# Two Strassen pairs for the query and key projection of the forgetting attention

## The reference, cut to what matters

```python
xn = rms_norm(h, norm_mix[i])
proj = jnp.einsum('bsd,de->bse', xn, w_in[i])
gdn_qkv, gdn_z, gdn_a, gdn_b, fox_qkv, fox_f, merge = split_cols(proj, IN_SPLITS)
...
q_f = rms_norm(fox_qkv[..., :FOX_W].reshape(B, S, FOX_HEADS, FOX_HD), q_norm[i])
k_f = rms_norm(fox_qkv[..., FOX_W:2 * FOX_W].reshape(B, S, FOX_HEADS, FOX_HD), k_norm[i])
v_f = fox_qkv[..., 2 * FOX_W:].reshape(B, S, FOX_HEADS, FOX_HD)
```

## Time and profile before

| | |
|---|---|
| median of 3 runs | 906.24 us (905.82 to 906.25) |
| profiled execution | 906.76 us, span 905.0 us |
| PE busy | 893.1 us, 99% of the span |
| DVE busy | 498.6 us, 55% |
| ACT busy | 198.1 us, 22% |
| DMA | 266 MB, 294 GB/s on the mean |

### The profile page before, as it was taken

One profiled execution on the slowest core, in us unless ns is written; L12 is line 12 of the kernel. 1 busy time (PEld: TensorE's weight loads), 2 busy tenths in 40 slices (PEclk: granted clock), 3 DMA queues, 4 the chain that ended last, 5 costly groups with the idle time before them and its releaser, 6 DMA issues.

```text
span 905.0 us, 21061 instructions
## 1 busy us (share of the span) xinstructions
PE 893.1 (99%) x9194; PEld 510.3 (56%) x9194; DVE 498.6 (55%) x954; ACT 198.1 (22%) x401; POOL 48.1 (5%) x72
## 2 busy tenths in 40 slices
PE   8999999999999999999999999999999999999997
PEld 6888755455845554446555555545455555555543
DVE  3656735964586887866434354443434444445367
ACT  2214200022417561233111111111111111111122
POOL 4011100050020000020000000000000000000010
PEclk9999999999999999999999999999999999999999
DMA  8643424562241528988999999999999999999951
GB/s 251 209 166 102 178 94 145 180 208 95 94 138 50 185 94 321 365 347 297 405 419 423 420 422 423 421 423 423 420 422 423 423 422 422 421 421 423 416 202 48
DMA packets 65587, 266.10 MB, mean 294 GB/s; under 512 B 11353, under 2 KB 14026, under 8 KB 41098
## 3 DMA queue, kind: packets, MB, share of 16 engines
q1 hardware_dynamic: 65530, 265.54, 74.4%
q10 hardware_dynamic: 16, 0.00, 0.0%
HBM read 263.69 MB, written 1.84 MB: 293 GB/s over the span
## 4 chain that ended last, share of the span: by engine, by line
PE 95%; DVE 2%; ACT 1%; issue 1%; DMA 0%; POOL 0%; DVEq 0%; ACTq 0%; POOLq 0%
PE bank L1493 25%; PE bank L1028 15%; PE bank L1474 13%; PE bank L1137 9%; PE bank L1018 9%; PE bank L1444 5%; PE bank L1457 5%; PE bank L1602 2%; PE bank L1005 2%; PE bank L1091 2%; PE bank L1513 1%; PE bank L1402 1%; PE bank L1413 1%; PE bank L1232 1%; PE bank L1330 1%; ACT arena L722 1%
## 5 line engine op out<-in xcount | busy, mean ns | idle before, releaser
L1493 PE MATMUL bank<-arena 128*32 128x256 f32 x4096 | 227.2, 379 | 0.3 <-DVE arena L2180 0.3
L1493 PEld LDWEIGHTS bank<-arena 128*32 128x32 f32 x4096 | 132.8, 110 | 100.5 <-issue 18.6
L1474 PE MATMUL bank<-arena 128*32 128x512 f32 x1024 | 116.5, 595 | 0.5 <-ACT arena L935 0.5
L1028 PE MATMUL bank<-arena 128*128 128x512 f32 x248 | 111.1, 598 | 0.0
L1137 PE MATMUL bank<-actT,arena 128*128 128x256 f32 x384 | 85.3, 380 | 0.0
L1018 PE MATMUL bank<-arena,actT 128*128 128x512 f32 x192 | 83.5, 593 | 0.0
L1137 PEld LDWEIGHTS bank<-actT,arena 128*128 128x128 f32 x384 | 72.0, 190 | 10.2 <-issue 0.8
L1028 PEld LDWEIGHTS bank<-arena 128*128 128x128 f32 x248 | 45.8, 190 | 53.9 <-issue 53.8
L933 ACT ACTIVATE arena<-bank 128x256 f32<-128x256 f32 x32 | 12.3, 384 | 267.9 <-PE bank L1493 267.9
L722 ACT ACTIVATE arena<-bank 128x512 f32<-128x512 f32 (+2 forms) x69 | 35.5, 534 | 154.5 <-PE bank L1018 82.7
L2231 DVE COPY arena<-bank 128x512 f32<-128x512 f32 x32 | 22.1, 692 | 81.9 <-PE bank L1474 81.9
(11 more groups left out here) (321 smaller groups left out, 1006.4 us busy)
## 6 DMA issues: line engine op xcount, KB each, us to landing
arena<-in_we_gate SPq DMA_DIRECT2D x32, 2048.0 KB, 17.3
arena<-in_we_up SPq DMA_DIRECT2D x31, 2048.0 KB, 18.5
arena<-in_we_down SPq DMA_DIRECT2D x29, 2048.0 KB, 17.5
arena<-in_w_in SPq DMA_DIRECT2D x17, 2048.0 KB, 8.1
arena<-in_we_down SPq DMA_DIRECT2D x6, 1024.0 KB, 8.9
arena<-in_w_branch_gdn SPq DMA_DIRECT2D x2, 2048.0 KB, 7.8
arena<-in_w_branch_fox SPq DMA_DIRECT2D x2, 2048.0 KB, 8.9
arena<-in_w_out SPq DMA_DIRECT2D x2, 2048.0 KB, 10.0
```

Source lines behind the costliest of these rows:

```text
L1028: ins = t.matmul(o[:, :], lhs[:, c, :], rhs[:, c, :], start=fresh and c == 0, stop=c == HC - 1, skip_group_check=not fresh)
L1474: ins = t.matmul(bank[4 + j][i * CAP:i * CAP + CAP, :], hidT[:, c, i * CAP:i * CAP + CAP], d_in[s][:, i % 2, c * D + WT * j:c * D + WT * j ...
L1493: ins = t.matmul(bank[4][i * CAP:i * CAP + CAP, m * DE:m * DE + DE], xg[:, c, i * CAP:i * CAP + CAP], gu_in[s][:, m, i % 2, c * DE:c * DE ...
```

## The change

Tiles 6 to 9 (queries and keys) become two pairs, `f0` and `f2`. The 8 blocks `fox.0.0` to `fox.3.1` go; 14 half products come, in the order of `FOX_ORDER`, with the same small jobs beside them. They take their banks from three, the small jobs from the other five. The sums' storage lies where other data is dead at that time (`RZ`, and `xi`'s place `TX`, so that POOL clears `xi` only after f2's last product). The token sums, before made after the solve for z, are made before f0. DVE's list is put in another order: the sums and additions of f0 between the `kk`, `bb` and `qk` scalings, three additions of f2 inside the solve, the scalings of q and k and the squares (`fox_squares`) behind it. SP requests tile 13 (z's second) ahead of `unbox_inverses` instead of behind it.

```diff
-BESIDE_FOX = {(0, 0): ["tq.0.5", "tq.1.5", "kk.0", "kk.1"], (0, 1): ["bbT", "kk.2", "kk.3"],
...
-PAIRED = ("z", "m0", "m2", "ya", "yf", "wo")
...
+FOX_BANKS, SIDE_BANKS = (7, 1, 2), (4, 5, 6, 0, 3)
+FOX_ORDER = (("f0", 1, ["tq.0.5", "tq.1.5", "kk.0", "kk.1"]), ("f0", 2, []), ("f0", 5, ["bbT", "kk.2", "kk.3"]), ("f0", 6, []),
+             ("f0", 3, ["bb.0", "bb.1", "bb.2", "bb.3"]), ("f0", 7, ["qk.0", "qk.1"]), ("f0", 4, []),
+             ("f2", 1, ["qk.2", "qk.3"]), ("f2", 5, []), ("f2", 2, []), ("f2", 6, []), ("f2", 3, []), ("f2", 7, []), ("f2", 4, []))
+
+PAIRED = ("f0", "f2", "z", "m0", "m2", "ya", "yf", "wo")
...
+        def sums_made(p, k):
+
+            return 4 * p + ((1, 2, 4, 3) if p < Z_ else (1, 3, 2, 4)).index(k) + 1
+
...
@@ SP
             for t in range(3, len(wtiles) - 1):
                 if t == W_FOX + 5:
                     box_blocks()
-                if t == W_PAIRED + 1:
+                if t == W_Z + 2:
                     unbox_inverses()
                 load(t)
...
@@ POOL
-            g.memset(xi[:, :, :], 0.0).then_inc(zeroed, 1)
             g.memset(vi[:, :, :], 0.0).then_inc(zeroed, 1)
...
+            wait_filled(pool, "f2.D")
+            g.memset(xi[:, :, :], 0.0).then_inc(zeroed, 1)
...
@@ ACT
-            for j in range(6):
-                for n in range(NT):
-                    drain(f"fox.{j}.{n}", fox[:, n, WT * j:WT * j + WT])
...
+            keep(F0_, 0)
+            drain("f0.A", result(F0_, 0, 0))
+            keep(F0_, 1)
+            wait_filled(act, "f0.D")
+            keep(F2_, 0)
+            keep(F2_, 1)
+            drain("f2.A", result(F2_, 0, 0))
+            for j in (4, 5):
+                for n in range(NT):
+                    drain(f"fox.{j}.{n}", fox[:, n, WT * j:WT * j + WT])
...
@@ PE
-            for j in range(6):
+            for pair_name, k, names in FOX_ORDER:
+                product(PAIRED.index(pair_name), k)
+                for name in names:
+                    beside(name)
+            for j in (4, 5):
                 w = weights(W_FOX + j)
                 for n in range(NT):
                     project(f"fox.{j}.{n}", w, n)
-                    for name in BESIDE_FOX.get((j, n), []):
-                        beside(name)
...
@@ DVE
+            values(0)
+            dve.wait_ge(qkss, 8)
+            weight_sum(F0_, 1)
+            values(1)
+            token_sums(LEFT[F0_])
+            dve.wait_ge(qkrinv, 8)
...
+            split(1, bk_split)
+            weight_sum(F0_, 2)
+            dve.wait_ge(d_masked, 8)
+            scaled_products("kk", lT, 0)
+            scaled_products("kk", lT, 1)
...
+            weight_sum(F0_, 4)
+            scaled_products("kk", lT, 2)
+            scaled_products("kk", lT, 3)
+            weight_sum(F0_, 3)
+            join(F0_, 6)
+            join(F0_, 3)
...
+            join(F0_, 7)
+            scaled_products("qk", dT, 0)
+            scaled_products("qk", dT, 1)
+            join(F0_, 4)
+            weight_sum(F2_, 1)
+            weight_sum(F2_, 2)
+            scaled_products("qk", dT, 2)
+            scaled_products("qk", dT, 3)
+            weight_sum(F2_, 4)
+            weight_sum(F2_, 3)
+            join(F2_, 6)
...
+            JOINED = {9: 3, 16: 7, 22: 4}
             for k in range(BLK - 1):
...
+                if k in JOINED:
+                    join(F2_, JOINED[k])
...
+            join(Z_, 6)
+            fox_normed(0)
+            for k in (3, 7, 4):
                 join(Z_, k)
+            fox_normed(1)
```

More of the change, by code:

```diff
@@ L80, in bank_fills @@
     f += ["tq.0.4", "tq.1.4"]
-    for j in range(6):
-        for n in range(NT):
-            f += [f"fox.{j}.{n}"] + BESIDE_FOX.get((j, n), [])
+    g = [(name, ALL_BANKS) for name in f]
+    for name, k, beside in FOX_ORDER:
+        if k in OPENS:
+            g += [(f"{name}.{OPENS[k]}", FOX_BANKS)]
+        g += [(b, SIDE_BANKS) for b in beside]
+    f = [f"fox.{j}.{n}" for j in (4, 5) for n in range(NT)]
     f += ["cT", "P5", "z.A", "X5", "V5", "z.C", "P6.0", "P6.1", "V6.0", "V6.1", "z.B", "z.D"]
@@ L373, in program @@
         wtiles = [(w_in2, C_QKV + WT * t, f"qkv.{2 * t + 1}") for t in range(6)]
-        wtiles += [(w_in2, C_FOX + WT * j, f"fox.{j}.1") for j in range(6)]
+        wtiles += [(w_in2, C_FOX + WT * j, f"fox.{j}.1" if j > 3 else f"f{j // 2 * 2}") for j in range(6)]
         wtiles += [(w_in2, C_Z + WT * j, "z") for j in range(2)]
@@ L457, in load @@
                 q = t - A_SLOTS
-                if q >= W_PAIRED and (q - W_PAIRED) % 2 == 0:
-                    p = (q - W_PAIRED) // 2
+                p, second = PAIR_OF.get(q, (None, None))
+                if p is not None and not second:
                     sp.wait_ge(half_filled, 3 * p + 3)
-                    sp.wait_ge(t_made, 4 * p + 4)
-                elif q >= W_PAIRED:
+                    sp.wait_ge(t_made, sums_made(p, 4))
+                elif p is not None:
                     wait_filled(sp, f"{wtiles[q][2]}.B")
@@ new lines, in _ @@
+            weight_sum(F0_, 4)
[4 more added lines that the diff above has]
+            join(F0_, 3)
+            for j in range(4):
+                nm = f"bb.{j}"
+                wait_filled(dve, nm)
+                wait_drained(dve, f"kk.{j}")
+                l4 = lT[:, 4 * j:4 * j + 4, :]
+                close(v.tensor_tensor(l4, l4, blocks4(nm), ALU.mult), nm)
+            join(F0_, 7)
+            scaled_products("qk", dT, 0)
@@ new lines, in _ @@
+            for k in range(BLK - 1):
+                m = BLK - 1 - k
+                outer = rank1[:, 0:m * (k + 1)].rearrange("p (i j) -> p i j", i=m)
+                seq(v.tensor_tensor(outer, bc(lb[:, k, k + 1:BLK], 2, k + 1), bc(xb[:, k, 0:k + 1], 1, m), ALU.mult))
+                below = xb[:, k + 1:BLK, 0:k + 1]
+                seq(v.tensor_tensor(below, below, outer, ALU.subtract))
+                if k in JOINED:
+                    join(F2_, JOINED[k])
+            v.tensor_copy(vblk.rearrange("p (j i) -> p j i", j=BLK), xblk.rearrange("p (i j) -> p j i", i=BLK)).then_inc(solved, 1)
@@ new lines, in _, with fox_squares @@
+            v.tensor_tensor(k0, k0, bc(et_s[:, 0:8], 2, P), ALU.mult).then_inc(scaled, 1)
+            for p in (F0_, F2_):
+                for q in "ACBD":
+                    wait_drained(dve, f"{PAIRED[p]}.{q}")
+            dve.wait_ge(c11_made, F2_ + 1)
+            def fox_squares(n, half):
+                src = fox[:, n, D * half:D * half + D]
+                seq(v.tensor_tensor(at(TPB, 1024), src, src, ALU.mult))
+                ins = v.tensor_reduce(f_ss[:, n, 16 * half:16 * half + 16], at(TPB, 1024).rearrange("p (a b) -> p a b", a=16), AX.X, ALU.add)
+                if half:
+                    ins.then_inc(fss, 1)
+                    dve.wait_ge(fss, n + 1)
+                else:
+                    seq(ins)
@@ L1898, in _ @@
+            fox_squares(0, 0)
+            fox_squares(0, 1)
             weight_sum(Z_, 1)
@@ L1921, in key_decays, with fox_normed @@
                     close(v.tensor_tensor(dst[:, :, 2 * P:3 * P], src[:, :, P:S], bc(negm[:, :], 1, 2), ALU.add), nm)
-            for n in range(NT):
+            def fox_normed(n):
                 dve.wait_ge(frinv, n + 1)
```

120 lines of the change are left out of this document (41 added, 79 removed).

## The result

The changed kernel takes 901.46 us (median of 5 runs, 900.49 to 902.66) against 906.24 us. The ratio is 0.9950, 95% interval 0.9938 to 0.9962, so it is faster by 4.8 us. The forecast was 901.4. Two later comparisons of the same two kernels gave 4.4 and 4.0 us. The profiled execution has a span of 900.9 us, 4.1 less than the 905.0 of before.

What follows compares the result with a forecast made beforehand. TensorE (PE), busy 893.1 of 905.0 us, bounds the kernel. Profiled 906.76 - 6.87 (matmuls) + 2.0 (wait) + 0.1 (DVE) = 902.0; as a median 906.24 - 4.8 = 901.4 us, range 899.2 to 904.1.

Steps and rivals of the forecast that it cites:

- The matmuls: Query and key blocks of the attention's projection: 64 matmuls become 56, saving 8 x 0.858 = 6.87 us.
- F: Moment PE could start P5, the first product needing the inverse's boxes back from memory: 196.35 before, 189.5 forecast without waits.
- DVE inside the pairs: Weight sums and additions, 25.2 us, fit beside PE in f0 and f2; thinnest margin 0.4 us, at f0's product 7.
- The 0.1 us that I charged: Loss allowed for the thinnest DVE margin, 0.4 us, at f0's product 7.
- The solve: DVE's small triangular solve starts at 152.2, 0.1 us later, holds four additions and ends at 178.6, 2.7 us later.
- The gap before P5: PE waits 2.0 us for the boxes' read-back, home at 191.5 against 189.5; with the ends 0.1 to 4.6 us.
- the boxes' tail: Time X and V land behind tile 13: 1.8 us taken, between 0.2 and 3.6 us.
- the boxes of 178.6 stand behind it in the same queue: X and V, solved at 178.6, wait in SyncE's queue behind tile 13, issued at 175.7; in memory at 185.6.
- The rule of the Trainium skill: Descriptors are consumed in ring order on each DMA engine; taken strictly, the time would be 0.6 us above that taken.
- rival 4: Gap before P5 lowers PE's clock to half; up to z's product 2 it costs 12.8 us: 914.2; chance 0.04.
- Rival 3: PE gets 5 us ahead but the experts' stage, bound by transfers, takes it back: 906.2; chance 0.06.
- a margin of 10.3 us: Before the change the inverse's boxes were home from memory at 186.0, 10.3 us before PE reached P5.

Runs made afterwards that it cites:

- the version without a wait at P5: Changed kernel with f2's addition for product 6 moved behind the solve's sixth step and tile 13 requested behind the read-backs; 899.60 us, repeated 898.85 us.
- ACT's queue: Changed kernel with X's and V's writing and read-back issued by ACT in its own DMA queue, tile 13 staying in SP's; 902.47 us.

## Why the prediction was right, and where it was not

- **The matmuls: right.** 6.87 us was the term. From the stage's start to F the old trace has 92.30 us and the new one 85.43: 6.87 less. One pair alone took 3.44 us off that stretch, and the version without a wait at P5 gained 6.6 us twice.
- **DVE inside the pairs: right.** PE has no wait between 103 and 188 us. The addition for product 6 ended at 125.8, PE reached product 7 at 126.5; the margin was 0.7 us, and 0.4 had been worked out. The 0.1 us that I charged wasn't spent. DVE's busy time from 104 to 152 us rose from 20.0 to 40.8 us.
- **The solve: right.** It was to start 0.1 us later than before, at 152.2, and to end at 178.6; less this execution's 0.6 us that is 151.6 and 178.0, and it was 151.66 and about 178.2.
- **The gap before P5: right in place and size.** 2.0 us were forecast; the profiled executions of the changed kernel and of its two repeats show 2.1, 1.4 and 1.7 us. F, the tile's issue at F - 13.85 and the boxes' tail of 1.2 us (forecast 1.8) behind a tile of 8.6 us (forecast 8.1) are all in the trace. The last two are off by 0.5 and 0.6 us and cancel.
- **Its cause: half wrong.** The step was "the boxes of 178.6 stand behind it in the same queue". ACT's queue gave the same landing. What delays them is a tile under way in the DMA engines; the order in the queue adds 1.0 to 1.5 us only when both are asked for together. The rule of the Trainium skill that I weighed there ("DMA: Bandwidth & Descriptors", "Queues, rings and completion order": consumption in ring order) holds for one ring, and no run contradicts it, but it isn't what decided.
- **A missing term: the clock.** I had it as rival 4, with 12.8 us or nothing, and a chance of 0.04. It does happen, in one of the changed kernel's three profiled executions, and costs 1.65 us there, not 12.8. The argument against it, one idle stretch of 0.85 us at full clock, was too thin for a gap of twice that length. From the first block of the stage to the end of z the three traces have 121.20, 119.13 and 120.49 us, the old one 124.61: 3.4, 5.5 and 4.1 less, 4.3 on the mean. That is -6.87, +1.8 for the gap, +0.6 for the clock and +0.2 for stalls among the X5 and V5 products (1.2 us in one trace), where I had -6.87 + 2.0 + 0.1. The three measured gains are 4.8, 4.4 and 4.0. That the first one, on which the forecast was measured, came out at the figure is partly luck: an unforeseen clock term was hidden by the spread of the start and of the gap.
- **Rival 3 (the experts' stage takes it back): wrong.** 676.3 us behind z in both traces.
- What stays open: in how many executions the clock falls behind P5, why it fell behind one idle stretch of 1.7 us and not behind another, and how the DMA engines divide themselves between two queues.

## What to carry to other kernels

When work is taken from an engine that is busy all the time, look for the chains through memory that it was hiding, and write down for each when it ends against the moment at which that engine will now arrive; here a margin of 10.3 us became a wait of about 2. A request that is moved ahead of another doesn't save a wait if both need the same DMA engines; find the slack in what starts them, as here in an addition that stood ahead of the solve for no need. And count a gap of about 2 us on TensorE not only by its length: the matmuls behind it can run at half clock.

## What the runs showed of the hardware that was not expected

- Of eight idle stretches of PE of 1.59 to 2.57 us in the thirteen traces seven were followed by 3.4 us (twice 6.8) at a granted clock of 0.50, which costs half of that; of thirteen of 0.6 to 1.56 us none was. With P5's gap cut to 0.8 us by idle transposes all five executions had a mean clock of 1.000. A mean clock of 0.997 doesn't say where such a fall was: three of the traces have it between 8 and 16 us.
- Boxes of 256 KB took 2.9 and 3.6 us alone, 5.4 and 6.1 with a 2 MB tile asked for 3.2 us ahead, 7.7 and 7.8 with one 0.7 us ahead; in another engine's queue 5.3 and 6.0, and 6.3 and 6.8.
- Read-backs in pieces of 128 bytes behind a 2 MB tile stretched even their issue: 7.2 us for eight instead of 4.0.
